# Transposes of the recurrent heads moved ahead of two row tiles, five small loads moved from ScalarE's queue to SyncE's, and two bias pairs of the second layer prepared one program earlier

## The reference, cut to what matters

```python
def _mixers(hl, hc, w_in, w_out, na_rpb, ...):
    pl = hl @ w_in                                    # latent tokens
    na_l = _neighbourhood_attention(q, k, v, kc, vc, na_rpb)     # 8 heads: window bias from na_rpb
    rw_l, rw_c = _bi_rwkv7(...)                       # 2 directions of 4 heads, 256 columns
    cv_l = _conformer_conv(...)                       # 256 columns
    return concatenate([na_l, rw_l, cv_l]) @ w_out    # 512 + 256 + 256 = 1024 rows of w_out

# end of _bi_rwkv7, per direction:
outs.append((_head_norm(yd, gn_g, gn_b) + bonus) * g)   # mean and variance of each head of 64
out = outs[0] + outs[1]

# neighbourhood attention: logits of a head and a latent query
s_win = where(col_mask, s_win + bias, -inf)             # bias: 15 x 127 numbers per head
p = softmax(concatenate([s_win, s_ctx]))
```

## Time and profile before

| | before |
|---|---|
| median of three runs | 2705.4 us |
| the profiled execution | 2705.65 us |
| its span | 2703.8 us |
| PE busy | 2592.5 us (96%) |
| DVE busy | 1127.2 us (42%) |
| ACT busy | 394.5 us (15%) |
| POOL busy | 242.8 us (9%) |
| DMA, mean over the span | 216 GB/s |
| granted TensorE clock, mean | 0.991 |

### The profile page before, as it was taken

The page is one execution under the profiler, slowest core; times in us unless marked ns, Lnnn a source line. Parts: engine busy times, 40 slices in busy tenths (PEclk is TensorE's granted clock), DMA queues, the critical chain, the costliest instruction groups (busy, mean ns, idle before and its releaser), DMA issues. The chain is left out here.

```text
span 2703.8 us, 54343 instructions
## 1 busy us (share of the span) xinstructions
PE 2592.5 (96%) x23985; PEld 1665.5 (62%) x23985; DVE 1127.2 (42%) x2209; ACT 394.5 (15%) x901; POOL 242.8 (9%) x271
## 2 busy tenths in 40 slices
PE   8999999999988999999999988889999999999998
PEld 6667988854557768887486457773443444534434
DVE  3387466236775547785833566550010010000102
ACT  1220200113252221000011423230000000000000
POOL 0000000000024301221100013410000000000000
PEclk9999999999999999999999999999999999999999
DMA  7366466422220013443643140079999999999997
GB/s 254 122 209 212 140 232 219 158 97 71 85 56 3 34 62 113 152 141 114 233 164 125 63 117 3 3 284 346 416 411 417 409 412 417 411 413 415 409 418 284
DMA packets 189499, 584.19 MB, mean 216 GB/s; under 512 B 26000, under 2 KB 41100, under 8 KB 172890
## 3 DMA queue, kind: packets, MB, share of 16 engines
q1 hardware_dynamic: 161283, 510.41, 50.0%
q0 software_dynamic: 16016, 59.04, 6.2%
q10 hardware_dynamic: 11975, 11.35, 1.4%
HBM read 571.02 MB, written 9.76 MB: 215 GB/s over the span
## 5 line engine op out<-in xcount | busy, mean ns | idle before, releaser
L3107 PE MATMUL bank<-work 128*32 128x512 f32 (+1 forms) x4608 | 437.8, 539 | 1.4 <-DMA work<-in_moe_w_up 1.2
L1260 PE MATMUL bank<-normed,weight_ring 128*128 128x256 f32 (+2 forms) x1760 | 366.1, 369 | 17.1 <-DVE normed L1146 8.5
L1260 PEld LDWEIGHTS bank<-normed,weight_ring 128*128 128x128 f32 x1760 | 311.0, 193 | 70.7 <-issue 22.9
L3107 PEld LDWEIGHTS bank<-work 128*32 128x32 f32 x4608 | 150.2, 110 | 283.4 <-issue 277.1
L1260 PE MATMUL bank<-work,weight_ring 128*128 128x256 f32 (+2 forms) x1104 | 283.6, 417 | 4.4 <-PEq L2830 2.2
L713 PE MATMUL bank<-normed,weight_ring 128*128 128x512 f32 (+1 forms) x832 | 278.2, 494 | 0.0
L1260 PEld LDWEIGHTS bank<-work,weight_ring 128*128 128x128 f32 x1104 | 209.4, 192 | 75.7 <-issue 52.6
L245 DVE SCALAR_TENSOR_TENSOR work<-work,small 128x512 f32<-128x512 f32 x336 | 239.6, 755 | 18.9 <-DMA work<-in_mod_w 12.5
L3326 DVE TENSOR_TENSOR work<-bank,work 128x512 f32<-128x512 f32 (+1 forms) x48 | 27.0, 618 | 512.0 <-PE bank L3107 512.0
L713 PEld LDWEIGHTS bank<-normed,weight_ring 128*128 128x128 f32 x832 | 157.5, 190 | 118.5 <-issue 108.3
L3121 PE MATMUL bank<-work 128*32 128x256 f32 x3072 | 167.4, 379 | 0.0
(11 more groups left out here) (396 smaller groups left out, 2628.7 us busy)
## 6 DMA issues: line engine op xcount, KB each, us to landing
work<-in_moe_w_gate SPq DMA_DIRECT2D x64, 1024.0 KB, 19.5
work<-in_moe_w_down SPq DMA_DIRECT2D x64, 1024.0 KB, 12.8
work<-in_mod_w POOLq DMA_DIRECT2D x48, 1024.0 KB, 5.7
work<-in_moe_w_up SPq DMA_DIRECT2D x64, 768.0 KB, 13.6
weight_ring<-in_w_in SPq DMA_DIRECT2D x40, 1024.0 KB, 7.4
weight_ring<-in_moe_w_up SPq DMA_DIRECT2D x32, 1024.0 KB, 21.3
work<-in_moe_w_up SPq DMA_DIRECT2D x32, 1024.0 KB, 20.9
weight_ring<-in_moe_w_down SPq DMA_DIRECT2D x32, 1024.0 KB, 18.1
```

The source lines that it names most:

```text
L1260: last = nc.tensor.matmul(self.banks(gi)[j][:, to], w[:, k, j * P:(j + 1) * P], a, start=k0 + k == 0, stop=k0 + k == final)
L3107: last = nc.tensor.matmul(self.bank[3 * up + a][g * R:(g + 1) * R, 0:n].rearrange("p (b j) -> p b j", j=R), xg[:, a, k], w[:, g], start=k ...
```

## The change

Four edits:

1. In `Linear.tensor`, `HeadsOut.tensor` (the transposes with their wait for the normed rows) stands ahead of row tiles 6 and 7 instead of behind them. The wait for the gated result stays in front of row tiles 4 and 5. Both layers.
2. The loads of a `Linear` are issued by a function of their own. Where the block has more work for SyncE (`then`, the second layer's output projection), SyncE issues them, ahead of the expert tiles; otherwise ACT does as before.
3. The bias work becomes a class, `NeighbourBias`, with a number `early` of head pairs that are loaded and windowed in the projection's block: none in the first layer, two in the second. There SyncE issues the shape's load and eight bias loads behind all weight tiles of the block, and POOL clears `unbiased` and adds the window to two head pairs behind its side loads. The other two head pairs stay in the attention's block.
4. POOL clears `unbiased` after it has waited for the window's shape, where it did so before that wait.

```diff
--- before.py
+++ after.py
@@ Linear.tensor
                         parts = [[k for k in range(nk) if k0 + k not in late], [k for k in range(nk) if k0 + k in late]]
+                        if parts[1]:
+                            self.heads.tensor(pe)
                         for n_part, ks in enumerate(parts):
                             if n_part and ks:
-                                self.heads.tensor(pe)
                                 self.heads.wait_gated(pe)
@@ Linear
+    def load(self, eng):
+        for dst, src in self.loads:
+            eng.dma_start(dst, src).then_inc(self.landed.sem, 16)
+
     def scalar(self, act):
-        for dst, src in self.loads:
-            act.dma_start(dst, src).then_inc(self.landed.sem, 16)
         if self.heads:
@@ the new class
+class NeighbourBias:
+    def load(self, sync, first, end):
+        if first == 0 and end:
+            a = TABLE_AT["window"][0]
+            sync.dma_start(self.shape, self.pr.ins["tables"][:, a:a + GRID_W]).then_inc(self.shaped.sem, 16)
+        for n in range(first, end):
+            seen = self.seen[n].rearrange("p h (r c) -> p h r c", r=ROWS_APART)
+            for h in range(2):
+                for row in range(2):
+                    off = ((self.layer * 8 + 2 * n + h) * 15 + 5 - row) * 127
+                    sync.dma_start(seen[row * GRID_W:(row + 1) * GRID_W, h],
+                                   bass.AP(self.pr.rpb_dram, off, [[1, GRID_W], [127, ROWS_APART], [1, GRID_W]])).then_inc(self.landed[n].sem, 16)
+
+    def window(self, pool, first, end):
+        window = self.shape.unsqueeze(1).to_broadcast([P, 2 * ROWS_APART, GRID_W]) if end else None
+        if first == 0 and end:
+            pool.wait_ge(self.shaped.sem, self.shaped.at(16))
+            self.nc.gpsimd.memset(self.unbiased, 0.0)
+        for n in range(first, end):
+            pool.wait_ge(self.landed[n].sem, self.landed[n].at(16 * 4))
+            seen = self.seen[n].rearrange("p h (r c) -> p (h r) c", r=ROWS_APART)
+            self.nc.gpsimd.tensor_tensor(seen, seen, window, ALU.add).then_inc(self.windowed.sem, 1)
@@ Program.linear
             def _(sync):
                 self.load_weights(sync)
                 if then:
+                    run.load(sync)
                     then(sync)
...
             def _(act):
+                if not then:
+                    run.load(act)
                 run.scalar(act)
@@ Program.head_attention
                 def _(sync):
-                    sync.dma_start(*bias_in["shape"]).then_inc(shaped.sem, 16)
-                    for n_side, (_, loads) in enumerate(bias_in["sides"]):
-                        for dst, src in loads:
-                            sync.dma_start(dst, src).then_inc(pair_in[n_side].sem, 16)
+                    bias_in.load(sync, bias_in.early, 4)
                     self.load_weights(sync)
@@ Program.block_two, the projection's block
+            bias_in = NeighbourBias(self, layer, 0 if ctx else 2)
...
                     prep.gpsimd(pool)
                     last.gpsimd(pool)
+                    bias_in.window(pool, 0, bias_in.early)
...
                     self.load_weights(sync, WEIGHT_SLOTS - 2)
+                    bias_in.load(sync, 0, bias_in.early)
```

More of the change, by code:

```diff
@@ L1838, in load_first, with __init__, take @@
             sync.dma_start(self.place(j), self.source(j, 0)).then_inc(self.full[j].sem, 16)
+class NeighbourBias:
+    def __init__(self, pr, layer, early):
+        self.pr, self.nc, self.layer, self.early = pr, pr.nc, layer, early
+        self.seen = []
+        self.shaped, self.windowed = pr.counted("window_landed"), pr.counted("bias_windowed")
+        self.landed = [pr.counted(f"side_load{n}_landed") for n in range(4)]
+    def take(self, end):
+        ar = self.pr.arena
+        if end and not self.seen:
+            self.unbiased, self.shape = ar.take("unbiased", SEQ), ar.take("window", GRID_W)
+        for n in range(len(self.seen), end):
+            self.seen.append(ar.take(f"bias{n}", 2, ROWS_APART * GRID_W))
+            assert ar.used["unbiased"][0] < ar.used[f"bias{n}"][0]
+    def load(self, sync, first, end):
[18 more added lines that the diff above has]
+            self.nc.gpsimd.tensor_tensor(seen, seen, window, ALU.add).then_inc(self.windowed.sem, 1)
 class Program:
@@ L1962, in head_attention @@
         shaped, windowed = self.counted("window_landed"), self.counted("bias_windowed")
-        pair_in = [self.counted(f"side_load{n}_landed") for n in range(len(bias_in["sides"]) if bias_in else 0)]
+        pair_in = [self.counted(f"side_load{n}_landed") for n in range(4 if bias_in else 0)]
         with nc.Block() as block:
@@ L1975, in _ @@
                 def _(pool):
[L1976 to L1982, removed]
+                    bias_in.window(pool, bias_in.early, 4)
             @block.tensor
@@ L2718, in block_two @@
                 {0: lambda pe: last.wait_emptied(pe, len(down) - 2), 1: add_up, 3: entry.taken})
+            bias_in.take(bias_in.early)
             with nc.Block() as block:
@@ L2756, in block_two @@
             ar.free("restart", "w2a2", "g2")
-            unbiased = ar.take("unbiased", SEQ)
-            window = ar.take("window", GRID_W)
-            bias = [ar.take(f"bias{n}", 2, ROWS_APART * GRID_W) for n in range(4)]
-            assert all(ar.used["unbiased"][0] < ar.used[f"bias{n}"][0] for n in range(4))
-            first_window = TABLE_AT["window"][0]
-            sides = []
-            for n in range(4):
-                seen = bias[n].rearrange("p h (r c) -> p h r c", r=ROWS_APART)
-                loads = []
-                for h in range(2):
-                    for row in range(2):
-                        off = ((layer * 8 + 2 * n + h) * 15 + 5 - row) * 127
-                        loads.append((seen[row * GRID_W:(row + 1) * GRID_W, h],
-                                      bass.AP(self.rpb_dram, off, [[1, GRID_W], [127, ROWS_APART], [1, GRID_W]])))
-                sides.append((bias[n].rearrange("p h (r c) -> p (h r) c", r=ROWS_APART), loads))
-            bias_in = dict(sides=sides, zero=unbiased, shape=(window, ins["tables"][:, first_window:first_window + GRID_W]))
+            bias_in.take(4)
             pairs = []
```

## The result

The changed kernel took 2684.1 us, the median of four runs (2681.96 to 2689.76), beside 2707.9 us for the kernel before: ratio 0.992, 95% interval 0.989 to 0.995. Measured again in five rounds it took 2681.7 us (2680.42 to 2686.14) beside 2705.2: ratio 0.9918, interval 0.9904 to 0.9931. The forecast was 2682.5, that is 22.9 us less than before; measured are 23.8 and 23.5 less.

The account below looks back on a forecast made before the run. PE was taken to bound the kernel, with gains passed on: 5.3 + 3.0 + 7.2 + 5.0 + 2.4 = 22.9 us off 2705.4 gives 2682.5 us. Its own range was 2677 to 2688, chance 0.66.

Parts of the forecast that it names:

- first layer, idle time: First layer's output projection: transposes moved forward wait for nothing, row tiles 4 and 5 start 5.3 us earlier.
- first layer, clock: First layer's output projection: without the idle time the low clock behind it goes, 3.0 us gained, bounds 0 and 3.0.
- second layer, attention: Second layer's attention: early bias pairs let DVE start at 1601.6 instead of 1608.87, 7.2 us gained.
- second layer's output projection, idle time: Second layer's output projection: ACT freed of loads and transposes moved, row tiles 4 and 5 start 5.0 us earlier.
- second layer's output projection, clock: Second layer's output projection: the 0.60 clock behind the idle time goes, 2.4 us gained, with 0 as lower bound.
- Bound by PE, with gains passed on: Whole kernel: PE sets the pace nearly without waits between the changed places, so a gain at one passes on.
- rival A: Both output projections: the clock falls anyway, so the gain is only 17.5 us, 2688 us; chance 0.11.
- The fear for DVE in the projection's block: Second layer's projection: POOL's early additions could disturb DVE by 3.6 us, hidden because DVE's work ends 11 us early.
- The output projection's margin of half a microsecond: Second layer's output projection: normed rows come at 1769.1, just before PE ends row tiles 0 to 3 at 1769.68.
- rival B: Second layer's output projection: heads come late, stage 0.4 us slower and clock still falls; gain 15.1, 2690 us; chance 0.08.
- The stream: Expert stage: the weight stream has no clock time of its own; PE waits 2.6 us in the last item.
- Rival D: Expert stage: fewer PE pauses lower the clock; a fall to 0.97 costs 27 us, 2709.5 us; chance 0.04.

Follow-up runs that it names:

- the loads alone: Kernel before, with only the five small loads of the second layer's output projection moved from ACT to SyncE: 2704.2 us, ratio 0.9986.
- the bias alone: Kernel before, with only two bias pairs early in the second layer's projection block and POOL's clearing behind the shape's wait: 2700.9 us, ratio 0.9970.
- the transposes alone: Kernel before, with only the transposes moved ahead of row tiles 6 and 7 in both layers: 2697.8 us, ratio 0.9966.
- long pause: Changed kernel, with PE also waiting for nine extra ACT copies ahead of row tiles 4 and 5 in the first layer: 2693.5 us, one run.
- late stream: Changed kernel, with SyncE holding the first expert tile loads until the second layer's gated result is there: 2680.8 us, ratio 0.9905.
- small window additions: Changed kernel, with POOL adding the window to only 4 columns of one head for the third and fourth head pair: 2682.9 us, one run.

## Why the prediction was right

The forecast of 2682.5 lies between the two medians, 2684.1 and 2681.7. That it is so close is partly luck, since several of the terms below differ between profiles of the same code by more than that. Its terms, against the first profile of after:

| term | forecast | measured |
|---|---|---|
| first layer, idle time | 5.3 | 5.43 |
| first layer, clock | 3.0 | 2.98 |
| second layer, attention | 7.2 | 6.51 |
| second layer's output projection, idle time | 5.0 | 5.16 |
| second layer's output projection, clock | 2.4 | 2.36 |
| sum | 22.9 | 22.4 |

(2.98 is 980.04 - 962.42 = 17.62 us from row tiles 4 and 5 to the next group before, less 977.03 - 962.39 = 14.64 after.)

**Bound by PE, with gains passed on.** Right. The stages between and behind the edits kept their length but for the clock, which falls or stands by chance behind some short waits.

**The clock.** Right, and rival A falls: with the idle time gone the clock is 1.00 at both places, and a pause put back brings the low clock back (0.78 behind 4.43 us). The size was partly luck: the loads alone leave the first layer's wait at 5.27 us, and lose 1.50 us of clock behind it where the bias alone loses 3.06 (the group of 52 takes 16.30 and 17.86 against 14.80). One argument I had for it was too simple. The loads alone show a wait of 3.36 us with the clock at 1.00 behind it, so "it fell when PE had stood idle" is no rule for one wait of that length. And I left a third place out: behind PE's wait of 7.22 us in the second layer's attention the clock was 0.60. I had no term for it, and against the profile of before none was needed; against the two others with the same attention it would have been.

**The attention.** The mechanism was right, the size off by 0.7 against the profile of before (the stage of before itself came out 1.3 us longer in two other profiles). I let DVE start half a microsecond behind the scores, as soon as the first of four matmuls is done; it starts at 1.13, when two are done (four of the eight records). And I took nothing for POOL's additions, with -2.3 to +1.7 as ends. Two long scalings cost 1.86 us of DVE, of which 1.17 reach the stage; before, one of 1.75 and one of 0.89 lost 1.66. From DVE's start to the scan it is 27.27 us instead of 27.07: 0.2 against the change, and 0.5 from the start. The fear for DVE in the projection's block was sized rightly: L1044 and L1055 lost 1.61 + 1.55 = 3.16 us there, under the 3.6 taken, and the stage did not move.

**The output projection's margin of half a microsecond.** Right, and it was the point on which rival B hung: the transposes alone show that rival, a wait of 4.87 us where it had 5.1, but end 0.40 faster where it had 0.4 slower. The transposes take 1.04 us and not the 0.95 taken, which is too little to matter.

**The stream.** Right in its conclusion, wrong in one reading. I said that PE waits 2.6 us for weights in the last item. The waits of PE over the expert stage of before list 1.2 us for the tiles; the 2.6 was the last item's extra length. Another 0.8 us of it are six matmuls (L3129) that items one to seven do not have, and the rest was not followed up.

**Rival D.** The expert stage's clock is 1.00, its items 108.44 us as before.

What no term held is small and mostly chance: 1.7 us at the wait in the dense part (it went the changed kernel's way in both its profiles), 0.86 and 1.54 against it in the first profile's scan and router (the router's stage is 127.07 to 127.77 us in six profiles of ten and 129.3 in the other four, by the clock). The end is 0.65 us longer in all seven profiles with the loads on SyncE (12.97 to 13.02 against 12.33 to 12.37 in the three without). The rows up to the last stores are the same in both. What it is stays open.

## What to carry to other kernels

Count a wait of the critical engine twice, once for itself and once for the clock behind it, and read the second from the granted clock of the windows: here it was 5.3 of 22.4 us. It differs between profiles of the same code, so take it from more than one. When work is moved ahead of the work that covered its inputs, look for who makes these inputs and what stands in that engine's list; in the second layer the reordering gained 0.4 us without the moved loads and they 4.1 without it, but 7.5 together. Judge a kernel with such a clock by stage lengths of several profiles, since a single execution differs by 10 us before the changed part has begun.

## What the runs showed of the hardware

- Three table loads of a few hundred bytes a partition took 7.75 us to issue on ACT while SyncE issued 1 MB tiles, and 1.52 us on SyncE ahead of these tiles. It is not ACT that is slow: at two other places of the kernel before (478.30 and 1280.45 us) three table loads took 1.45 and 1.63 us to issue on ACT. So the issue time of a load is not its own. That SyncE's eight tiles, issued from 1762.64 on, are the cause is argued from what stood beside it; no run moved only them.
- POOL's addition slows some operations of DVE and not others. Scalings went from 0.49 to between 0.63 and 1.75 us, a product of two on-chip operands (L1044) from 1.22 to 2.83; the operation with the bias (one operand from the matmul's bank) kept its 0.68 to 0.69 in every profile. POOL loses too where DVE's are long: two additions took 4.46 to 5.30 us in the projection's block, about 1.8 each in the attention's. The order counted here: with the long pause L1044 began 0.37 us ahead of POOL's addition and took its 1.22, where in the changed kernel it began 0.80 behind it and took 2.83. The Trainium skill (SBUF — State Buffer, section "SBUF: two separate sides") limits the shared port's lock to operations of DVE in a two-port mode or with two operands in SBUF. The trace agrees: L1044 has two such operands, and the one with a bank operand is never held. The scalings have a single operand there, and no view here shows in which mode they ran.
- Whether the clock falls behind a short wait differs between profiles of the same instructions. Behind 2.35 us the same sixteen matmuls took 3.69 us in five profiles and 5.2 to 5.4 in five. Behind the 2.23 us at the start of the first layer's dense down block the clock was 0.72 or 0.73 over 6 us in eight profiles and 1.00 in two (late stream, small window additions), and these two took 321.20 us to the attention instead of 322.9. Behind a wait of 1.9 us in the second layer's projection it fell in one of ten (long pause: 0.62 over 4 us, 1.6 us lost). A wait of 1.17 us cost nothing in addition, and one of 3.36 nothing in the one profile that has it. Waits of 4.43 to 5.27 did in all five profiles that have one, though not the same: 1.50 to 3.06 us. The Trainium skill (TensorE: Matmul & The Clock Gate, section "Part 1: The HAM clock gate (the "warmup" mystery)") calls the number of slow matmuls at a kernel's start run-variable for one and the same kernel. The traces here show the same kind of spread in the middle of a kernel.
